# Moving gate products into the state-space scan, a value projection ahead of the convolution, and one head's work ahead of the attention loop

## The reference

```python
u = hn @ w_in
y_a = mla_branch(u_mla, cos, sin, ...) @ w_br_mla      # rotary attention, 8 heads
y_b = fox_branch(u_fox, ...) @ w_br_fox                # attention with a forget gate, 8 heads
y_c = ssm_branch(u_ssm, ...) @ w_br_ssm                # conv, state-space scan, gated norm by silu(z)
g = sigmoid(u_gate + b_gate).reshape(B, S, 3, D)
merged = g[:, :, 0] * y_a + g[:, :, 1] * y_b + g[:, :, 2] * y_c
x = x + merged @ w_out
x = x + conv_ffn(rms_norm(x, norm_ffn_g), ...)
```

## Time and profile before

| | us |
|---|---|
| median of 3 runs | 2308.07 (2300.03 to 2327.18) |
| the profiled execution | 2319.43 |
| its span | 2317.7 |
| TensorE busy in it | 2175.5 (94%) |
| VectorE busy | 1133.9 (49%) |
| ScalarE busy | 814.7 (35%) |
| GpSimd busy | 132.3 (6%) |

### The profile page before, as it was taken

The page is one execution under the profiler, slowest core; times in us unless marked ns, Lnnn a source line. Parts: engine busy times, 40 slices in busy tenths (PEclk is TensorE's granted clock), DMA queues, the critical chain, the costliest instruction groups (busy, mean ns, idle before and its releaser), DMA issues.

```text
span 2317.7 us, 24798 instructions
## 1 busy us (share of the span) xinstructions
PE 2175.5 (94%) x10133; PEld 1794.5 (77%) x10133; DVE 1133.9 (49%) x1649; ACT 814.7 (35%) x1154; POOL 132.3 (6%) x115
## 2 busy tenths in 40 slices
PE   5989988998999999999999998979999999999996
PEld 5877876977888778888777776768888878888875
DVE  3734455374343456536535878452344444334235
ACT  4455642423232243313332352543233243123232
POOL 0000000010000000000003950000000000000000
PEclk9998899988999999999999999989999999999998
DMA  3221012200322333233233202212232223223221
GB/s 117 82 73 37 1 37 66 90 1 19 109 92 91 127 91 91 92 106 94 73 96 122 91 20 70 85 37 91 91 107 94 91 79 103 91 92 108 92 100 55
DMA packets 166495, 185.58 MB, mean 80 GB/s; under 512 B 4711, under 2 KB 129894, under 8 KB 166382
## 3 DMA queue, kind: packets, MB, share of 16 engines
q1 hardware_dynamic: 162568, 174.96, 23.8%
q10 hardware_dynamic: 3110, 6.90, 0.8%
q0 software_dynamic: 704, 2.13, 0.3%
HBM read 181.86 MB, written 2.12 MB: 79 GB/s over the span
## 4 chain that ended last, share of the span: by engine, by line
PE 87%; DVE 6%; ACT 4%; issue 1%; DMA 1%; ACTq 0%; POOL 0%; DVEq 0%; POOLq 0%
PE ps L334 25%; PE ps L335 25%; PE ps L336 25%; PE ps L426 3%; PE ps L446 2%; PE ps L329 2%; PE ps L437 1%; ACT arena L1097 1%; DVE WL L1535 1%; PE ps L409 1%; PE ps L614 1%; PE ps L642 1%; PE ps L460 1%; ACT WH L1068 0%; DVE X L2007 0%
## 5 line engine op out<-in xcount | busy, mean ns | idle before, releaser
L1535 DVE TENSOR_TENSOR WL<-W,WH 128x2048 fp32r<-128x2048 f32 (+2 forms) x168 | 378.6, 2259 | 490.0 <-ACT WH L1068 468.2
L334 PE MATMUL ps<-HH,WH 128*128 128x512 f32 x1416 | 556.3, 393 | 11.1 <-DVE HL L1558 6.4
L335 PE MATMUL ps<-HL,WH 128*128 128x512 f32 x1416 | 553.3, 391 | 0.0
L336 PE MATMUL ps<-HH,WL 128*128 128x512 f32 x1416 | 553.2, 391 | 0.0
L1068 ACT ACTIVATE WH<-W 128x2048 fp32r<-128x2048 f32 (+2 forms) x168 | 314.2, 1876 | 319.9 <-DMA W<-in_w_ff_dram 109.6
L334 PEld LDWEIGHTS ps<-HH,WH 128*128 128x128 f32 x1416 | 267.3, 189 | 70.5 <-DVE WL L1535 7.8
L336 PEld LDWEIGHTS ps<-HH,WL 128*128 128x128 f32 x1416 | 267.2, 189 | 55.8
L335 PEld LDWEIGHTS ps<-HL,WH 128*128 128x128 f32 x1416 | 267.5, 189 | 55.5 <-issue 0.2
L334 PE MATMUL ps<-WH,arena_r 128*128 128x512 f32 (+1 forms) x616 | 240.7, 391 | 9.4 <-DVE WL L1535 6.4
L335 PE MATMUL ps<-WL,arena_r 128*128 128x512 f32 (+1 forms) x616 | 239.8, 389 | 0.0
L336 PE MATMUL ps<-WH,arena_r 128*128 128x512 f32 (+1 forms) x616 | 239.7, 389 | 0.0
(11 more groups left out here) (323 smaller groups left out, 2451.4 us busy)
## 6 DMA issues: line engine op xcount, KB each, us to landing
W<-in_w_in_dram SPq DMA_DIRECT2D x51, 1024.0 KB, 5.2
W<-in_w_ff_dram SPq DMA_DIRECT2D x32, 1024.0 KB, 5.2
W<-in_ffn_w_up_dram SPq DMA_DIRECT2D x44, 512.0 KB, 5.1
W<-in_w_gate_dram SPq DMA_DIRECT2D x16, 1024.0 KB, 4.9
W<-in_ffn_w_down_dram SPq DMA_DIRECT2D x10, 1024.0 KB, 5.0
W<-in_w_out_dram SPq DMA_DIRECT2D x8, 1024.0 KB, 5.0
W<-in_w_branch_dram SPq DMA_DIRECT2D x8, 1024.0 KB, 5.0
W<-in_w_br_ssm_dram SPq DMA_DIRECT2D x4, 1024.0 KB, 4.9
```

The lines of the kernel that those rows point to most:

```text
L334: pe.matmul(out_, st[0], mv[0], start=first, stop=False)
L335: pe.matmul(out_, st[0], mv[1], start=False, stop=False)
L336: return pe.matmul(out_, st[1], mv[0], start=False, stop=last)
L1535: dve.tensor_tensor(WL[:, j % RING, 0:n], W[:, j % RING, 0:n], plain(WH[:, j % RING, 0:n]), ALU.subtract).then_inc(slab_lo, 1)
```

## The change

**mla.** fsm is projected before fq, fk comes between the transposes of the queries and of the keys, then FT and fv, and only then the attention loop, which has no work of the other branch in it any more. The fox norms of queries and keys stand ahead of the loop too. VectorE copies the transposed keys out of PSUM (`dve_turn`), ScalarE the queries. **fox.** The slab of dtsm is projected here. **ssm.** z comes first, as two long products of 512 columns in four slabs; the decay rows are made beside it; xbc has three buffers in place of two and is transposed two tiles later. Two gate slabs follow, and nine more stand in the scan, two per chunk and one at its end; the products of `keep_clock` in the scan are gone. A rounded copy of the first two branches' rows lies in the memory of X. The output of the gating norm is written over the chunk's input. **gates1** has the remaining nine slabs. **convin, band, sgu.** The four projection slabs of convin alternate, GpSimd has no taps, VectorE does those of all four channel tiles (16 in convin, ten per slab in band, two in every three steps of its loop, 24 and a last 5 in sgu), and the norm of v stands ahead of the last five.

```diff
+    first, second = ([(n, *x) for x in branch_order(4)] for n in range(2))
+    order = first + second + [(2, *x) for x in branch_order(8)]
+    PRE_GATES = order[:2]
+    SCAN_GATES = [[x] for x in order[2:11]]
+    REST_GATES = order[11:]
...
 # TensorE, mla
-                gemm_t_long("fq", full, 672, hnt)
                 w = slab(KT, P, win(2208, 2208 + P))
                 gemm_f("fsm", w, KT, 0, 1, hn)
                 slab_read()
+                gemm_t_long("fq", full, 672, hnt)
                 pe.wait_ge(heads_ready, 1)
                 turn_heads("mla", "QT", at(7168, NT, HEADS, DQ), DQ)
+                gemm_t_long("fk", full, 1184, hnt)
                 pe.wait_ge(heads_ready, 2)
                 turn_heads("mla", "KT", at(10240, NT, HEADS, DQ), DQ)
+                pe.wait_ge(f_ready, 1)
+                b = bank("FT")
...
+                gemm_t_long("fv", full, 1696, hnt)
...
 # TensorE, ssm
+                gemm_t_long("z", full, 2216, hnt, 0)
+                gemm_t_long("z", full, 2728, hnt, 1)
...
-                        if 0 <= j - 1 < 10:
-                            turn_conv(j - 1)
+                        if 0 <= j - 2 < 10:
+                            turn_conv(j - 2)
                     slab_read()
...
+                for x in PRE_GATES:
+                    gate_slab("G1", *x)
...
                 for t in range(NT):
...
-                    keep_clock(b, KEEP["chunk"])
...
-                                keep_clock(b, KEEP["state"])
...
+                    for n, kind, cc, j in SCAN_GATES[2 * t]:
+                        gate_slab("G1", n, kind, cc, j)
                     pe.wait_ge(xdt_ready, t + 1)
...
-                            keep_clock(b, KEEP["mix"])
...
                             arow(3)
+                            for n, kind, cc, j in SCAN_GATES[2 * t + 1]:
+                                gate_slab("G1", n, kind, cc, j)
                             if t > 0:
                                 yturn(t - 1)
+                for n, kind, cc, j in SCAN_GATES[2 * NT]:
+                    gate_slab("G1", n, kind, cc, j)
                 yturn(NT - 1)
...
+            def gate_slab(tag, n, kind, cc, j):
+
+                gate, br, kt = branches(tag)[n]
+                if kind == "g":
+                    w = slab(KT, 256, gate(2 * cc + j))
+                    gemm_f((tag, "g", n, cc), w, KT, 0, 2, hn, 2 * j)
+                    slab_read()
+                    return
+                if cc == 0 and j == 0:
+                    ys_made[0] += kt
+                    pe.wait_ge(y_split, ys_made[0])
...
 # ScalarE, scan
                     if t > 0:
                         scale(t - 1)
+                    for n, kind, cc, j in SCAN_GATES[2 * t]:
+                        gate_out("G1", n, kind, cc, j)
                     decay(4 * t + 2)
                     decay(4 * t + 3)
+                    for n, kind, cc, j in SCAN_GATES[2 * t + 1]:
+                        gate_out("G1", n, kind, cc, j)
+                    if t == 2:
+                        rows_high("G1", 1)
...
 # VectorE, scan
                     mix(0)
                     mix(1)
+                    for n, kind, cc, j in SCAN_GATES[2 * t]:
+                        gate_sum("G1", n, kind, cc, j)
                     diff(2)
                     diff(3)
-                    if t > 0:
-                        keep(t - 1)
                     mix(2)
                     mix(3)
...
+                    diagonal(0)
+                    for n, kind, cc, j in SCAN_GATES[2 * t + 1]:
+                        gate_sum("G1", n, kind, cc, j)
+                    if t == 2:
+                        rows_low("G1", 1)
+                    if t > 0:
+                        keep(t - 1)
...
+                    diagonal(1)
...
 # VectorE, sgu
+                b = use(dve, "swT")
+                freed(dve.tensor_copy(swT, b[:, :].rearrange("p (g i) -> p g i", g=4)), "swT")
...
-                taps(DVE_CHANNELS * TAPS - tapped[0])
+                split(slab_of["su", 2])
                 rstd(stat[:, 0:4], 1)
...
+                taps(len(TAP_ORDER) - tapped[0])
                 split(slab_of["su", 3] + 1)
...
```

More of the change, by code:

```diff
@@ L821, in pe_sgu @@
                 tr.then_inc(pe_done, 1)
+                for j in range(2):
+                    w = slab(KT, 256, win(256 * j, 256 * j + 256, "w_in_2"))
+                    gemm_f("su", w, KT, 0, 2, hn, 2 * j)
+                    slab_read()
                 swT, v = at(12800, 4, P), at(10240, NT, 512)
@@ L1044, in _ @@
                     program[s]()
-                if s == "band":
-                    pool.drain().then_inc(gpsimd_end, 2)
-                    pool_conv()
-                elif s == "sgu":
-                    for end in (tensor_end, scalar_end, vector_end):
-                        pool.wait_ge(end, k + 1)
-                else:
-                    boundary(pool, gpsimd_end, k)
+                boundary(pool, gpsimd_end, k)
         @block.scalar
@@ L1224, in act_mla @@
-                attention("mla", 0, at(2048, 4, S), at(4096, 3, S), at(0, 4, S), beside_scores)
-            def softplus(v, a, ps_in, bias, scale, name):
-                freed(act.activation(v, ps_in, ACT.Identity, bias=bias, scale=scale), name)
+                taken(act, ("fq", NT - 1, 0))
+                fox_squares(Qa)
+                split(slab_of["fk", 0, 0] + 1)
+                root(stat2[:, 0:32])
+                for t in range(NT):
+                    b = result(("fk", t, 0))
+                    freed(act.activation(Ka[:, t, :, 0:HD], b[:, :].rearrange("p (h d) -> p h d", h=HEADS), ACT.Copy), ("fk", t, 0))
@@ new lines, in act_mla, with fox_squares @@
+                taken(act, ("fk", NT - 1, 0))
+                act.wait_ge(head_sums, 2)
+                fox_squares(Ka)
+                split(slab_of["fv", 0, 0])
+                root(stat2[:, 32:64])
+                for t in range(NT):
+                    b = result(("fv", t, 0))
+                    freed(act.activation(V2[:, t, :], b[:, :], ACT.Copy), ("fv", t, 0))
+                attention("mla", 0, at(2048, 4, S), at(4096, 3, S), at(0, 4, S))
+            def fox_squares(T):
+                Tv = T.rearrange("p t h d -> p (t h) d")[:, :, 0:HD]
+                act.activation(beside(2112, 3 * HEADS, HD), Tv[:, 0:3 * HEADS], ACT.Square)
+                act.activation(at(6656, HEADS, HD), Tv[:, 3 * HEADS:], ACT.Square).then_inc(head_squares, 1)
@@ L1229, in softplus @@
+            def softplus(v, a, name):
                 taken(act, name)
@@ new lines, in act_ssm, with rows_high @@
+                for n, kind, cc, j in SCAN_GATES[2 * NT]:
+                    gate_out("G1", n, kind, cc, j)
+            GATES = {"G1": ("b_gate", 0, 3), "G2": ("b_gate2", KT, 4)}
+            def rows_high(tag, n):
+                kt = 8 if (tag, n) == ("G1", 2) else 4
+                before = n - 2 if tag == "G2" else 0 if (tag, n) == ("G1", 1) else -1
+                if before >= 0:
+                    result(((tag, "b", before, 1), 3))
+                if (tag, n) == ("G1", 2):
+                    taken(act, ("yT", NT - 1, 1))
+                ys = split_rows(tag, n)[0]
+                for k in range(kt):
+                    act.activation(in_tiles(ys[:, k, :]), whole_row(tag, n, k), ACT.Copy).then_inc(hi_ready, 1)
@@ L1791, in fox_scale, with dve_turn @@
                 dve.tensor_tensor(Tv, Tv, bc(st.unsqueeze(2), [P, 32, HD]), ALU.mult).then_inc(heads_ready, 1)
+            def dve_turn(tag, dst, d, gcol):
+                for h in range(HEADS):
+                    b = use(dve, (tag, "KT", h))
+                    freed(dve.tensor_scalar(dst[0:d, h, :], b[0:d, :], gq[0:d, gcol:gcol + 1], None, ALU.mult),
+                          (tag, "KT", h))
             def dve_fox():
+                dve_turn("fox", at(19456, HEADS, S), 66, 3)
+                split(slab_of["dtsm", 0] + 1)
                 dve.wait_ge(mask_ready, 2)
@@ new lines, in gate_sum, with dve_gates1, dve_gates2 @@
+                if n == GATES[tag] - 1:
+                    merged_low(4 * cc + cs[-1])
+            def dve_gates1():
+                for n, kind, cc, j in REST_GATES:
+                    if (n, kind, cc, j) == (2, "g", 0, 0):
+                        rows_low("G1", 2)
+                    gate_sum("G1", n, kind, cc, j)
+            def dve_gates2():
+                for n in range(4):
+                    rows_low("G2", n)
+                    for kind, cc, j in branch_order(4):
+                        gate_sum("G2", n, kind, cc, j)
@@ L2160, in dve_convin @@
                     if c == 1:
+                        split(slab_of["cg", 2] + 1)
+                        taps(FIRST_TAPS)
                         dve.wait_ge(rel_tiles, 16 * HEADS)
```

560 lines of the change are left out of this document (257 added, 303 removed).

## The result

| | before | after |
|---|---|---|
| median | 2308.81 (2300.03 to 2327.18, 4 runs) | 2212.99 (2211.33 to 2217.19, 4 runs) |
| the profiled execution | 2319.43 | 2217.19 |
| its span | 2317.7 | 2215.5 |
| mean granted clock | 0.964 | 0.977 |

The ratio is 0.9601 [0.9567, 0.9634]: faster by 92 us by the ratio, by 95.8 between the medians and by 102.2 between the profiled executions. The forecast was 105 off the profiled execution and 2203 for the median. An execution that is over 1.5% longer than the fastest of its kernel is named with its experiment and left out of the ratio; there are two (experiments 7 and 11).

The account below looks back on a forecast made before the run. TensorE's own stream was taken as the bound. Terms of -26 (mla), -68 (ssm and gates1 with fox) and -11 (sgu) made -105 us: 2214 from the profiled 2319.43, 2203 against the median, range 2174 to 2250.

Parts of the forecast that it names:

- mla: Mla stage: transposes -7.2 us, a loop like that of fox -22.3, less three small waits; net -26, ends -29.5 and -7.
- fox: Fox stage: dtsm's 24 products come in, +5.5 us; its transposes and loop stay.
- ssm up to the scan: Ssm stage before the scan: z as two long projections and twelve shorter xbc tiles, 143.7 to 115.7 us, -28.0.
- scan and 11 slabs: Scan with eleven gate slabs, two before it: 221.4 to 169.0 us, -52.4, plus 7 for small waits.
- convin, band: VectorE takes over the fourth channel tile's taps: nothing gained or lost, ends 0 and +5 us.
- sgu: Sgu stage: the norm of v starts earlier under su and mixing keeps more clock; net -11 us, ends -12 and 0.
- What nobody reads: Scan: the 120 keep_clock products, whose results are unread, taken out as 27.3 us saved.
- VectorE as the bound of the scan: Rival: slab splits and sums burden VectorE's serial chain in the scan; half the nine slabs unhidden, 2245; chance 0.12.
- Low clock in the mla loop: Rival: the new mla loop stalls once and runs at the lower clock as before, +19 us, 2222; chance 0.07.
- The function sets: Rival: about 8 more ScalarE function-set loads in the scan lie on the chain, +10 us, 2213; chance 0.10.
- The scan losing its clock: Rival: without filling products the gate slabs fail to hold 2.4 GHz and scan work doubles, +42 us, 2350; chance 0.04.
- No overlap: Rival: the scan keeps its 101.2 us and the nine slabs come on top, -60 in all, 2248; chance 0.05.

Follow-up runs that it names:

- experiment 7: Kernel after without the 20 filling products ahead of each of the three attention loops: median 2202.27; ratio 0.9543 to before without the profiled execution of 2244.16.
- experiment 11: Kernel after with three weight slabs (fq's first, gv's second, gr's second) split earlier: ratio 0.9579 to before from three executions, a fourth of 3598.40 left out.
- experiment 2: Kernel before with VectorE norming v ahead of its last 19 taps, nothing else changed: 2314.42, ratio 1.0042 to before.
- experiment 3: Kernel before without the 120 keep_clock products in its scan, no slab moved: 2316.54, ratio 1.0056 to before.
- experiment 1: Kernel before with the mla part of the change alone: 2288.07, ratio 0.9925 to before.
- experiment 5: Kernel after with the 120 keep_clock products back in the scan beside the gate slabs: 2235.11, ratio 0.9696 to before.
- experiment 6: Kernel after with Identity in place of the sigmoid of the first two gates, so no sigmoid in the scan: 2215.77, ratio 0.9607 to before.
- experiment 4: Kernel after with the scan's nine gate slabs moved behind the scan, no filling: 2255.91, ratio 0.9784 to before.
- experiment 9: Kernel before with only fsm and its softplus moved ahead of fq: 2302.61, ratio 1.0001 to before.

## Why the prediction was right, and where it was not

The direction, the bound (TensorE's own stream) and the sum against the profiled execution held: -102.2 for -105. That it came so close is in part luck: some 13 to 16 us of it are lower clock in the one execution of before from which the forecast was read and against which -102.2 is taken, and in the scan two wrong terms cancel. The terms:

| term | forecast | profiled execution |
|---|---|---|
| mla | -26 | -26.0; against the mla stage of experiments 2 and 3, -14.4 and -15.2 |
| fox | +5.5 | +5.5 |
| ssm up to the scan | -28.0 | 143.7 to 115.2, -28.5 (z 7.3 less, twelve tiles 1.44 less each, dtsm 5.5 less, decay rows 1.5 more) |
| scan and 11 slabs | -52.4 + 7 | 221.4 to 175.5, -45.9; with the 96.71 us scan of experiment 2, -41.4 |
| convin, band | 0 | 0 |
| sgu | -11 | -11.7 |
| not forecast | | wout1 +1.7, gla +1.8 |

- **mla: the mechanism was right, its size was off for the median.** The step that failed is "without its two projections 115.21 - 43.72 = 71.5 us for the same 32 steps": it took one execution's low stretch, 23.90 us at 0.50, for a property of the loop. Two other executions of the same code show the stage 10.8 and 11.6 us shorter (215.4 and 214.6), and experiment 1 gives the part 11.5 to 23 us. The prediction then took the 11.4 us between the profiled execution and the median off the result as if it were the same for both kernels. It was not: the profiled execution was long in the old mla loop and, by 2 to 5 us, in the old scan, and the change replaces both. That is the 10 us by which 2203 was missed. Of the waits that the term counts, fq's first slab was 1.00 us late (1.5 forecast), and the one before fk was 1.49 us (1.3); the 64 transposes took 7.24 us busy in two pieces (near 7 forecast). That the loop holds its clock once it enters as fox does was right: with nothing in it, it held 1.00 in all ten profiles taken. Whether the stall of 1.23 us ahead of the old stretch is what brought the clock down was argued and not tested; the same stall stands ahead of the 3.41 us one.
- **The scan: right sum, one term for the wrong reason.** The +7 stood for small waits where three chains meet. There are none, TensorE's idle time is 0.00. In their place came 17.1 us at the lower level, a loss of 8.5. And the 48.8 us of real work were 46.7 (153.62 less nine slabs, 98.4, less 8.5), as 1.5 of them moved beside z. 46.7 + 120.2 + 8.5 makes the 175.5 that were measured, and 48.8 + 120.2 + 7 made 176.0 forecast: that agreement is luck. The slabs held the clock up except for these five stretches.
- **"What nobody reads" was half right.** The prediction counted 27.3 us of filling products as plain loss, in the kernel before. Experiment 3 refutes that there: taking them out alone costs 13 us, and half of them lay in waits. They became waste only once slabs did their work, where experiment 5 prices them at 22. The sum came right because the prediction also took out the 14.2 us of lost clock, which only the slabs give back; and experiment 3 shows that without slabs the clock is lost with the filling.
- **sgu** came as forecast, but "the norm starts as soon as sv is read" leaves out what lets it: experiment 2 shows that VectorE's order alone gives nothing and costs 10 us. The prediction has eight steps that hold "the first gla slab" by 1.4 us; it is the second, and TensorE's wait for it went from 1.07 to 2.03.
- **convin and band.** 0 forecast, 0 measured. A tap took 744 ns in the mean without GpSimd's, for 996.
- **"From the first z product to the last gate product some 383 us"** was a slip: 463 with the prediction's own -73.4 gives 390, and 389.8 was measured. The lower end of its range, 2174, is 5 below what its own terms give (2187 less 8).
- **The rivals.** VectorE as the bound of the scan: refuted, TensorE waits for nothing there and 27.3 us more of products came out as 22 to 26. Low clock in the mla loop: absent in all profiles of the new loop. The function sets: refuted by experiment 6, with eight loads fewer and 0 us. The rows have a load at 1.28 us, and ScalarE is busy for 67.23 of 153.62 us. The Trainium skill ("ScalarE: Activation LUTs", section "What ACT_TABLE_LOAD costs") prices a switch at 2.66 us; that price too stays off the chain here, so its advice to batch by set did not decide this order. The scan losing its clock: real as a mechanism (experiments 3 and 4, clocks of 0.58 and 0.64), averted by the slabs. No overlap: refuted by experiment 4, the overlap is worth 42 to 43 us.

Not settled: how much of fsm's move shows in the median (experiment 9), how the 11.7 us of sgu divide among its moves, and why the old mla loop now and then keeps the lower level for 24 us rather than 3.4. The 28.5 us ahead of the scan had no experiment of their own; they are read from the windows.

## What to carry to other kernels

Before a stretch at the lower clock goes into a forecast as a property of the code, compare at least two executions of it; the difference between the profiled execution and the median may sit in just that stretch. Useful dense work interleaved with short products pays twice, for the waits it fills and for the clock it holds (here 14.6 and 26 us), and only once it was there were the filling products waste. When an engine's step is moved earlier, move what it waits for on the other engines as well, or the work that it was moved past lands on the next stage.

## What the runs showed of the hardware

- TensorE fell to 1.2 GHz without idle time before it: five times in the scan of the kernel after (idle time 0.00 in 153.62 us), each time at a run of short products. In the band loop of experiment 7 it stayed there for 88.75 us in which it was busy throughout, behind a wait of 0.78 us. The Trainium skill ("TensorE: Matmul & The Clock Gate", section "What's actually happening") ties the level to how busy the array has been of late and lists 1.2 GHz as the idle state. By the profile's busy time (3.41 of 3.41 us, and idle time 0.00 ahead of it) the idle state is not what these falls show; whether the chip's own measure of busy is another, no run here tells.
- The same code keeps a different clock in different executions: one low stretch of the mla loop lasted 23.90 us in one and 3.41 in another, the scan of after had 17.1 us at the lower level in its own profile and 27.3 in that of experiment 11, and the kernel of experiment 7 ran at 2194.45 and at 2244.16.
- 120 products that nobody reads saved 13 us in one order of the work and cost 22 in another.
- A tap of VectorE (128x512) took 1257 ns in the mean beside GpSimd's elementwise work, and 0.67 us alone.
